# The first projection phase takes x turned by the host, with its norms spread by TensorE

## The reference, cut to what matters

```python
def rms_norm(x, w):
    y = x * lax.rsqrt(jnp.mean(x * x, axis=-1, keepdims=True) + NORM_EPS)
    return y * w

u = rms_norm(h, norm_w[layer])                      # (1, 2048, 1024)
proj = jnp.einsum('bsd,dc->bsc', u, w_in[layer])    # (1, 2048, 4096)
hg_q, hg_f, hg_i, hg_z, at_q, at_k, at_v, at_z = jnp.split(proj, split_points, axis=-1)
```

## Time and profile before

| | |
|---|---|
| median of the runs | 1278.96 us |
| the profiled execution, its own time | 1280.67 us |
| its span, first to last instruction | 1278.9 us |
| mean granted TensorE clock | 0.992 |
| busy: TensorE, VectorE, ScalarE, GpSimd | 98%, 55%, 36%, 34% |
| the prologue's first product, and the copy behind its last one | 15.7 us, 82.0 us |

### The profile page before, as it was taken

How to read it: one execution, slowest core, us unless ns; L and a number is a source line. 1 busy time by engine, 2 the same in 40 slices (tenths; PEclk the granted TensorE clock), 3 DMA queues, 4 the chain that set the end, 5 groups by cost and what they waited for, 6 DMA issues and landing times.

```text
span 1278.9 us, 24337 instructions
## 1 busy us (share of the span) xinstructions
PE 1248.3 (98%) x8944; PEld 1090.0 (85%) x8944; DVE 704.3 (55%) x1933; ACT 460.3 (36%) x1328; POOL 436.2 (34%) x441
## 2 busy tenths in 40 slices
PE   7999999999999999999999999999999998999997
PEld 7989999999999989999888888888888876888886
DVE  5847877887766797111455444544554545333332
ACT  5631222222222212112555555554554546421121
POOL 5543254343534413122153345333533434021000
PEclk8999999999999999999999999999999998999999
DMA  6520122211221212341455466545545666544431
GB/s 213 175 90 19 55 63 81 77 59 59 63 79 59 75 67 76 96 116 48 125 141 141 122 143 152 134 116 148 147 125 140 161 179 181 160 145 143 148 116 66
DMA packets 121717, 143.94 MB, mean 113 GB/s; under 512 B 20352, under 2 KB 86400, under 8 KB 121600
## 3 DMA queue, kind: packets, MB, share of 16 engines
q1 hardware_dynamic: 117024, 134.26, 36.9%
q10 hardware_dynamic: 4576, 8.13, 2.3%
HBM read 87.56 MB, written 29.62 MB: 92 GB/s over the span
## 4 chain that ended last, share of the span: by engine, by line
PE 88%; DVE 3%; DMA 3%; issue 1%; POOL 1%; ACT 1%; SPq 1%; ACTq 0%; POOLq 0%; DVEq 0%
PE bank L665 11%; PE bank L667 11%; PE bank L666 11%; PE bank L837 6%; PE bank L836 6%; PE bank L835 6%; PE bank L863 5%; PE bank L865 5%; PE bank L864 5%; PE bank L927 3%; PE bank L936 3%; PE bank L991 3%; PE bank L998 3%; PE bank L760 2%; PE bank L964 2%
## 5 line engine op out<-in xcount | busy, mean ns | idle before, releaser
L665 PE MATMUL bank<-w_hi,u_hi 128*128 128x256 f32 x768 | 221.3, 288 | 3.3 <-DVE u_lo L1472 2.4
L666 PE MATMUL bank<-w_lo,u_hi 128*128 128x256 f32 x768 | 218.2, 284 | 0.0
L667 PE MATMUL bank<-w_hi,u_lo 128*128 128x256 f32 x768 | 218.1, 284 | 0.0
L665 PEld LDWEIGHTS bank<-w_hi,u_hi 128*128 128x128 f32 x768 | 148.1, 193 | 5.1 <-DVE u_lo L1472 3.9
L666 PEld LDWEIGHTS bank<-w_lo,u_hi 128*128 128x128 f32 x768 | 148.2, 193 | 0.1
L667 PEld LDWEIGHTS bank<-w_hi,u_lo 128*128 128x128 f32 x768 | 148.1, 193 | 0.0
L1472 DVE TENSOR_TENSOR room<-room 128x256 f32<-128x256 f32 (+6 forms) x386 | 130.9, 386 | 16.7 <-POOL room L1357 10.7
L835 PE MATMUL bank<-u_hi,w_hi 128*128 128x512 f32 x256 | 107.8, 421 | 0.5 <-issue 0.5
L1472 DVE TENSOR_TENSOR t<-bank,tab 128x512 f32<-128x512 f32 x64 | 42.4, 684 | 116.6 <-DMA tab<-in_rope 52.7
L836 PE MATMUL bank<-u_lo,w_hi 128*128 128x512 f32 x256 | 101.9, 398 | 2.7 <-DMA far_v<-values 2.7
L665 PE MATMUL bank<-u_hi,w_hi 128*128 128x512 f32 x256 | 103.0, 402 | 0.6 <-ACT sg_tile L1093 0.6
(11 more groups left out here) (169 smaller groups left out, 2846.9 us busy)
## 6 DMA issues: line engine op xcount, KB each, us to landing
qd<-turned SPq DMA_DIRECT2D x64, 256.0 KB, 4.5
stage<-in_w_groups SPq DMA_DIRECT2D x42, 256.0 KB, 4.0
room<-in_x SPq DMA_DIRECT2D x16, 512.0 KB, 3.9
values_gates<-vg_tile SPq DMA_DIRECT2D x64, 128.0 KB, 1.7
room<-values_gates SPq DMA_DIRECT2D x16, 512.0 KB, 3.9
tab<-in_rope SPq DMA_DIRECT2D x16, 512.0 KB, 4.5
wide<-mix_weights SPq DMA_DIRECT2D x32, 256.0 KB, 3.9
xr<-in_x SPq DMA_DIRECT2D x16, 512.0 KB, 4.9
```

Of the source, the lines that this page charges most:

```text
L665: yield nc.tensor.matmul(dst, lhs_hi(k), rhs_hi(k), start=(k == 0), stop=False)
L666: yield nc.tensor.matmul(dst, lhs_hi(k), rhs_lo(k), start=False, stop=False)
L667: last = nc.tensor.matmul(dst, lhs_lo(k), rhs_hi(k), start=False, stop=(k == KT_N - 1))
```

## The change

The host gives x a second time, as `x_turned`: for each tile 128 features by 8 blocks by 128 tokens, already turned. SyncE loads that as well (512 KB a tile; the first four tiles singly, then pairs of 1 MB into three slots `xT`). The rows of x are still loaded, for the squares only. TensorE's eight transposes of a tile are replaced by one, which turns the column of 128 inverse norms, broadcast to 128 columns, so that each partition of a PSUM bank holds the norms of all tokens (`spread_norms`). VectorE multiplies x_turned by gain and norms in one instruction per block (`scaled` for a tile: 8 of 128x128; `scaled_pair` for two: 8 of 128x256). From tile 4 on squares and norms come in pairs, and ScalarE itself asks for the rows of x from tile 6 on, each behind the square that frees the slot. The host's work is a change of layout.

```diff
 SyncE
+            load_turned(0) ... (1), (2), (3) between the loads of x and the pieces of weights
+            for t in range(2):
+                after(xsq_done, t + 1)
+                load_x(t + X_SLOTS)
+            load_pair(2)
             sp.dma_start(tri, tri_masks).then_inc(tri_landed, 16)
-            for step in range(TILES + 5):
-                if step >= 5:
-                    phase1_store(0, step - 5)
-                if step - 3 in SPLIT_AT:
-                    load_piece(1, SPLIT_AT.index(step - 3))
-                if step + X_SLOTS < TILES:
-                    after(xn_done, step + 1)
-                    load_x(step + X_SLOTS)
+            for t in range(TILES):
+                if t % 2 and t // 2 + XT_SLOTS < PAIRS:
+                    after(ulo_done, t + 1)
+                    load_pair(t // 2 + XT_SLOTS)
+                if t - 1 in SPLIT_AT:
+                    load_piece(1, SPLIT_AT.index(t - 1))
+                if t >= 1:
+                    phase1_store(0, t - 1)
 TensorE
+            def spread_norms(t, many):
+                pe.wait_ge(rstd_done, t + many)
+                for z in range(t, t + many):
+                    last = nc.tensor.transpose(rstd_row(z), rstd[:, z:z + 1].to_broadcast([P, P]), ident[:, :])
+                last.then_inc(rows_done, many)
             for t in range(TILES):
-                if 1 <= t < TILES - 2:
-                    x_transposes(t + 2)
                 pe.wait_ge(ulo_done, t + 1)
                 matmuls = phase1_tile(0, t, "prologue")
+                run(itertools.islice(matmuls, 16 if t == 0 else 12))
+                if t < 2:
+                    spread_norms(t + 2, 1)
+                elif t < 4:
+                    spread_norms(2 * t, 2)
+                elif t % 2 == 0 and t + 5 < TILES:
+                    spread_norms(t + 4, 2)
                 run(matmuls)
 ScalarE
+            def square(t):
...
+                if 2 <= t < TILES - X_SLOTS:
+                    act.wait_ge(xsq_done, t + 1)
+                    act.dma_start(xt[t % X_SLOTS], x[(t + X_SLOTS) * P:(t + X_SLOTS + 1) * P, :])
+            square(0)
+            split_hi(0, 0, 0)
+            square(1)
+            for i in range(1, PIECES):
+                split_hi(0, i, 0)
+            square(2)
+            for t in range(1, TILES + 2):
+                if t == 2:
+                    phase1_tile(0, 0, "prologue")
+                if t < TILES:
+                    high_parts(t)
+                for z in {4: (6, 7), 5: (8, 9)}.get(t, (t + 2 if t < 4 else t + 4,)):
+                    if z < TILES:
+                        square(z)
+                if t >= 3:
+                    phase1_tile(0, t - 2, "prologue")
 VectorE
+            def scaled_pair(q):
+                slot = xT[q % XT_SLOTS]
+                dve.wait_ge(xT_landed[q % XT_SLOTS], 16 * ((q - 2) // XT_SLOTS + 1))
+                dve.wait_ge(rows_done, 2 * q + 2)
+                for k in range(KT_N):
+                    last = nc.vector.scalar_tensor_tensor(out=slot[:, :, k, :], in0=slot[:, :, k, :], scalar=nw[:, k:k + 1],
+                                                          in1=rstd_rows_of_pair(q), op0=ALU.mult, op1=ALU.mult)
+                last.then_inc(un_done, 2)
+            for t in range(SINGLE):
+                scaled(t)
+                if t == 0:
+                    dve.wait_ge(un_done, 1)
+                    nc.vector.tensor_copy(u_hi[:, :, 0:P], xT[0][:, 0]).then_inc(uhi_done, 1)
+                low_parts(t)
+            scaled_pair(2)
+            for q in range(2, PAIRS):
+                if q == 2:
+                    low_parts(4)
+                    low_parts(5)
+                if q + 1 < PAIRS:
+                    scaled_pair(q + 1)
+                if q > 2:
+                    low_parts(2 * q)
+                    low_parts(2 * q + 1)
```

More of the change, by code:

```diff
@@ L26 @@
 X_SLOTS = 4
+XT_SLOTS = 3
+SINGLE = 4
+PAIRS = TILES // 2
 Q_SLOTS = 3
@@ L205, in build @@
         p2.at = (3 * P + 2 * HG_UNITS + 2 + 3 * HG_UNITS + 16 + (HG_UNITS + 1) * P + P)
-        xn = [p2.take(D) for _ in range(2)]
+        xT = [p2.take(2, KT_N, P) for _ in range(XT_SLOTS)]
         xsq = p2.take(D)
-        un = [p2.take(KT_N, P) for _ in range(2)]
         xt += [p2.take(D) for _ in range(2)]
         ss, rstd = p2.take(TILES), p2.take(TILES)
+        assert p2.at <= p.at - 2 * D
         z_hi = at("z_hi", W_AT, [KT_N, P], F32R)
@@ L291, in build @@
         x_landed0, x_landed1, xsq_done = sem("x_landed0"), sem("x_landed1"), sem("xsq_done")
[L292 removed]
+        rstd_done, rows_done = sem("rstd_done"), sem("rows_done")
+        xT_single = [sem(f"xT_single{t}") for t in range(SINGLE)]
+        xT_landed = [sem(f"xT_landed{i}") for i in range(XT_SLOTS)]
         un_done, uhi_done, ulo_done = sem("un_done"), sem("uhi_done"), sem("ulo_done")
@@ new lines, in scaled @@
+            def scaled(t):
+                turned_x = xT[t // 2][:, t % 2]
+                dve.wait_ge(xT_single[t], 16)
+                dve.wait_ge(rows_done, t + 1)
+                for k in range(KT_N):
+                    last = nc.vector.scalar_tensor_tensor(out=turned_x[:, k, :], in0=turned_x[:, k, :], scalar=nw[:, k:k + 1],
+                                                          in1=rstd_row(t), op0=ALU.mult, op1=ALU.mult)
+                last.then_inc(un_done, 1)
+            def scaled_pair(q):
+                slot = xT[q % XT_SLOTS]
+                dve.wait_ge(xT_landed[q % XT_SLOTS], 16 * ((q - 2) // XT_SLOTS + 1))
+                dve.wait_ge(rows_done, 2 * q + 2)
+                for k in range(KT_N):
+                    last = nc.vector.scalar_tensor_tensor(out=slot[:, :, k, :], in0=slot[:, :, k, :], scalar=nw[:, k:k + 1],
+                                                          in1=rstd_rows_of_pair(q), op0=ALU.mult, op1=ALU.mult)
+                last.then_inc(un_done, 2)
```

147 lines of the change are left out of this document (65 added, 82 removed).

## The result

Four executions of the changed kernel take 1294.92 us in the median (1291.12 to 1297.47), against 1278.66 us for the kernel before, run beside them: a ratio of 1.0128, interval 1.0096 to 1.0161, **about 16 us slower**. The profiled execution took 1297.47 us, its span is 1295.7 us, against 1280.67 and 1278.9. The forecast was 1282.2 in a range that ended at 1290. The direction and the places were right, the size was five times too small.

A forecast was written before the change was run, and what follows sets the result against it. TensorE, 88% of the chain, was taken as the bound, with VectorE near its limit in the prologue. Prologue end 86.7 against 82.0, 4.7 late, less 1.5, gave 3.2 us slower: 1278.96 to 1282.2 us, range 1273 to 1290.

The forecast's parts named there:

- the scaling: VectorE's paired 128x256 instruction in the prologue: 0.40 us each, 3.2 us a pair, with no delay added for GpSimd.
- the walk: Step through four lists of the prologue, each step starting when engine and inputs are ready: end at 86.7 against 82.0 us.
- From there the norms are ahead: From tile 7 at 57.7 us on, no more waits for norms: nine tiles at 3.2 us, ending at 86.7.
- The correction: 1.5 us taken off the prologue's 4.7 us loss, because the kernel before came out at 83.5 against 82.0 traced.
- Up to tile 7: Prologue until tile 7 begins: at 57.7 us against 48.8 before, 8.9 late, through waits for weights and norms.
- The piece for tile 1: First piece of group 1's weights, needed by ScalarE: lands about 33.6 us, behind other loads in full DMA engines.
- the rate: Loading in the prologue while DMA engines are full: 0.41 MB per us.
- The piece for tile 4: Weights asked for after tile 3's store and pair 5: landing at 52.0 us, ScalarE waiting 4.6 us.
- Behind tile 7: Rest of the prologue: nine tiles at 3.2 us, 5.9 us a pair plus low parts behind GpSimd's, ending at 86.7.
- B: Rival: weights land in time and only the prologue's serial start remains: 1277 us, within 1274 to 1280; chance 0.22.
- C: Rival: norms always in front, TensorE never stops; 2.5 us from the start, 9 from transposes: 1267 us; chance 0.10.
- D: Rival: paired scaling nearer 0.48 us makes VectorE the bound, or clock falls in gaps: 1287 to 1292 us; chance 0.15.

The follow-up runs named there:

- e4: The kernel before, also given the turned x as an input that nothing reads: 1277.55 us, ratio 1.0005.
- e10: The kernel before with 105 idle transposes (11.3 us) on TensorE between prologue and rest: 1288.77 us, ratio 1.0088.
- e8: The changed kernel with 30, 42 and 50 unread transposes filling TensorE's gaps in tiles 2, 3 and 6: 1293.1 us, ratio 1.0114.
- e9: The changed kernel with weights asked for early and 9.2 MB less of x loaded (from pair 3 and tile 6 on): 1283.06 us, ratio 1.0059.
- e7: The changed kernel with weights asked for early, exponential last, squares earlier and VectorE scaling one tile ahead: 1279.02 us, ratio 1.0018.

## Why the prediction was right in direction and wrong in size

**Right.** First product at 13.2 said, 13.5 measured; tile 1 at 19.9, and 20.0 measured; tile 2 at 25.3, and 24.4 measured; the DMA engines full until 33 said, 35 measured; the scaling at 0.40 said, 0.39 measured; TensorE idle inside tiles 3 and 6, released by norms, and ScalarE at the weights of tiles 1 and 4. Neither event that I named as refuting it came: the weights of tile 4 landed at 54.7, not before 48, and the spread for 6 and 7 ran at 40.7, not before 36. I put no delay on the scaling, because the gain instruction, with one operand in PSUM, had kept its time whatever stood beside it. The scaling took 3.22 us in every pair, both for the pair at 30.54 us, with GpSimd idle from 30.60 on, and for the one at 42.68, with GpSimd at work from 44.25 on. The Trainium skill (SBUF — State Buffer, "Who interferes with whom") says that a VectorE instruction with at most one input in SBUF does not contend with GpSimd (outside the modes with two ports), and the trace agrees.

**Wrong, by term of the sum.** The mechanism was right as far as the walk followed it. The step that failed is "From there the norms are ahead": the walk stopped at tile 7, while ScalarE stood at two more pieces of weights; before it, the landings of the first two pieces were sized too early, and after it 1.5 us were taken off without a ground. In the prologue the forecast was 3.2 us and the profile has 10.9. The missing 7.7 are:

- *The correction, 1.5 us.* I took 1.5 us off, because the same walk was that much too long for the kernel before. That step had no ground. Its size rests on one profile: in e4 and e10 the same prologue ends at 79.8 us, not 82.0. And the walk had been too long where the old order has cover; in the new order, a chain from engine to engine with little cover, fixed costs count in full, as I now read it (no run tests this). Uncorrected, the walk said 86.7; the profile has 92.86.
- *Up to tile 7, 4.1 us (61.8 measured, 57.7 said).* The piece for tile 1 was cast at 35.3 and not at 33.6, because 12.3 MB had moved by then and not 11.4 (pair 4, asked for at 31.00 us, is not in my count); the rate was right (406 GB/s measured, 410 said). The piece for tile 4 came 2.7 us later than said, at 54.7. Each lateness went through ScalarE's list and the norms to TensorE in full: the spreads ran at 40.7 and 58.75, said 38.8 and 56.0. The last 1.3 are the twelve products behind the spread at the lower level; that is where the time stands, not a loss that a higher clock gives back, since e8 begins tile 7 only 0.35 us earlier.
- *Behind tile 7, 2.1 us (31.1 for nine tiles, 29.0 said).* I walked no further, at 3.2 us a tile. ScalarE stood at two more pieces, 3.88 and 2.29 us, and VectorE waited 2.09 us for pair 6, which SyncE, behind a store that waits, asked for only at 62.53 us:

```profile
62.53 1.16 SPq L452 DMA_DIRECT2D room<-in_x_turned  x1
```

```profile
68.81 3.22 DVE L1552 SCALAR_TENSOR_TENSOR room<-room,nw,bank 128x256 f32<-128x256 f32 x8 [2.09 <-DMA room<-in_x_turned]
```

The first of the two rows is SyncE's timeline, the second VectorE's. The other 5.9 us of the span lie behind the prologue; there I had forecast nothing, and in e10 a later start alone brought nothing on top. That part is open.

Two sums of the forecast are slightly off as they stand: nine tiles at 3.2 us are 28.8 and end at 86.5, not 86.7, and with 358 GB/s put into the sum for the first piece it lands at 36.1 us, not near 37. Neither changes the forecast.

**The rivals.** B's price is refuted by e9, with the reserve given there: with weights in time and the loads cut from pair 3 on the prologue still ends at 84.6, where B put it some 2 us ahead of 82.0. It takes another order on VectorE as well to come near that (e7, 78.84). C never came near. D named a right fact and a wrong price: the clock did fall, in four stretches, and holding it up in e8 brought nothing that these runs can measure; its other half, a dear scaling, did not come. My range ended at 1290 because D was its upper end; what was missing in it was the forecast's own mechanism, carried on to the last piece.

On loading, the trace moved 403 to 406 GB/s from 12 to 34 us where the Trainium skill (DMA: Bandwidth & Descriptors, "Where 436 GB/s comes from") has about 358 per core; the trace decides, as it did in the earlier trace rows. What the forecast missed on loading was not the rate, but bytes that moved ahead of or beside a piece, and requests that came late.

## What to carry to other kernels

When a change adds loads to a stretch whose DMA engines are already full, look for the small loads and stores queued in that stretch: here 256 KB of weights took 11.6 us to land, and asking for four such pieces earlier, with not a byte saved, halved the loss (1.0128 to 1.0064 of the time before). In the repaired versions a 128 KB store held a copy for up to 7 us. Walk such a chain to its end, with every later instance of the same wait, and take no correction off a walk for a kernel that has cover which the new one has not. And an order of one engine's list is good or bad only together with the others': the same reordering of VectorE ended the prologue 6.4 us earlier with weights early and 4.5 us later with weights late.

## What the runs showed of the hardware that I had not expected

- An exponential between two sigmoids cost a table load of 1.28 us on either side, with the next activation 1.29 and 1.30 us behind the load's start. Ahead of the first sigmoid, before, it had none of its own.
- Idle transposes that hold the granted clock at 1.00 through gaps of 3.6 to 6.2 us bought nothing in the end of the prologue (93.38 against 92.86 us, single profiles that scatter by some 2 us).
- A 256 KB load asked for at 23.67 us landed 11.64 us later: 4.7 MB were moved in that time, at 402 to 416 GB/s.
